# Hybrid decoder layer: the 31-tap depthwise convolution computed by the parity of tokens

## The reference

```
u = conv_val * sigmoid(conv_gate)                      # (B, 2048, 512)
u = causal_depthwise_conv(u, conv_w, conv_b)           # 31 taps, left padded, one filter per channel
uf = u.reshape(B, S, 4, 128)                           # 4 groups of 128 channels
uf = (uf - mean(uf)) * rsqrt(var(uf) + EPS)            # over the 128 channels of a group
y_conv = silu(uf * conv_norm_w + conv_norm_b)
```

## Time and profile before

| | |
|---|---|
| median of 3 runs | 2086.41 us (2086.11 to 2086.6) |
| the profiled execution | 2085.33 us, of which 2083.5 us are the span from the first to the last instruction |
| PE busy | 2067.1 us, 99% |
| DVE busy | 1446.1 us, 69% |
| ACT busy | 912.1 us, 44% |
| POOL busy | 417.2 us, 20% |

### The profile page before, as it was taken

One profiled execution on the slowest core, in us unless ns is written; L12 is line 12 of the kernel. 1 busy time (PEld: TensorE's weight loads), 2 busy tenths in 40 slices (PEclk: granted clock), 3 DMA queues, 4 the chain that ended last, 5 costly groups with the idle time before them and its releaser, 6 DMA issues. The chain is left out here.

```text
span 2083.5 us, 26901 instructions
## 1 busy us (share of the span) xinstructions
PE 2067.1 (99%) x10031; PEld 1734.2 (83%) x10031; DVE 1446.1 (69%) x1993; ACT 912.1 (44%) x1557; POOL 417.2 (20%) x252
## 2 busy tenths in 40 slices
PE   9999999999999999999999999999999999999998
PEld 8897878878788888788888888888788888888887
DVE  6897999989567777886666976666563536624285
ACT  6632434343454445754555654455331313313163
POOL 0000000000002323352332333232353134400012
PEclk9999999999999999999999999999999999999999
DMA  5121212113656875765446755545756455543376
GB/s 204 32 87 47 70 41 81 51 32 105 199 177 195 266 235 171 266 192 167 137 142 191 236 171 156 167 150 189 245 210 259 154 193 202 174 169 126 138 257 218
DMA packets 254144, 338.55 MB, mean 162 GB/s; under 512 B 11584, under 2 KB 195648, under 8 KB 240192
## 3 DMA queue, kind: packets, MB, share of 16 engines
q1 hardware_dynamic: 221376, 315.80, 45.6%
q10 hardware_dynamic: 32384, 20.98, 3.2%
q0 software_dynamic: 256, 0.07, 0.0%
HBM read 225.58 MB, written 111.21 MB: 162 GB/s over the span
## 5 line engine op out<-in xcount | busy, mean ns | idle before, releaser
L1978 PE MATMUL psum<-x_hi,w_hi_P 128*128 128x512 f32 x896 | 349.8, 390 | 3.8 <-DVE x_lo L1922 2.4
L2198 PE MATMUL psum<-w_hi,hid_hi 128*128 128x512 f32 x896 | 348.8, 389 | 1.9 <-DVE hid_lo L2074 1.9
L1978 PE MATMUL psum<-x_lo,w_hi_P 128*128 128x512 f32 x896 | 349.1, 390 | 0.0
L1978 PE MATMUL psum<-x_hi,w_lo_P 128*128 128x512 f32 x896 | 349.1, 390 | 0.0
L2198 PE MATMUL psum<-w_hi,hid_lo 128*128 128x512 f32 x896 | 348.6, 389 | 0.0
L2198 PE MATMUL psum<-w_lo,hid_hi 128*128 128x512 f32 x896 | 348.6, 389 | 0.0
L2074 DVE TENSOR_TENSOR hid_lo<-hid_raw,hid_hi 128x1024 fp32r<-128x1024 f32 x112 | 174.4, 1593 | 211.4 <-ACT hid_hi L2069 211.4
L1891 POOL TENSOR_TENSOR w_raw<-w_raw 128x512 f32<-128x512 f32 x128 | 184.9, 1467 | 395.3 <-DVE w_lo_P L1904 345.8
L2069 ACT ACTIVATE hid_hi<-hid_raw 128x1024 fp32r<-128x1024 f32 x112 | 112.9, 1051 | 343.4 <-DMA hid_raw<-scratch_hid 343.3
L1904 DVE TENSOR_TENSOR w_lo_P<-w_raw,w_hi_P 128x512 fp32r<-128x512 f32 x224 | 184.1, 834 | 98.1 <-ACT w_hi_P L1900 95.5
L1900 ACT ACTIVATE w_hi_P<-w_raw 128x512 fp32r<-128x512 f32 x224 | 136.0, 626 | 236.8 <-PE psum L1978 227.2
(11 more groups left out here) (284 smaller groups left out, 3820.0 us busy)
## 6 DMA issues: line engine op xcount, KB each, us to landing
scratch_hid<-stage SPq DMA_DIRECT2D x224, 256.0 KB, 3.7
hid_raw<-scratch_hid SPq DMA_DIRECT2D x56, 1024.0 KB, 4.9
w_raw<-in_w SPq DMA_DIRECT2D x52, 1024.0 KB, 5.0
w_grain<-in_w SPq DMA_DIRECT2D x48, 512.0 KB, 5.3
x_raw<-scratch_h2s SPq DMA_DIRECT2D x14, 1024.0 KB, 8.4
w_raw<-in_w_in SPq DMA_DIRECT2D x22, 512.0 KB, 3.6
scratch_h2s<-h2s SPq DMA_DIRECT2D x8, 1280.0 KB, 10.1
scratch_qk<-qout ACTq DMA_DIRECT2D x16, 512.0 KB, 3.3
```

The lines of the kernel that those rows point to most:

```text
L1978: mm = nc.tensor.matmul(psum[:, bank_1(op, g), :], l, r, start=kt == 0 and i == 0, stop=kt == 3 and i == 2)
L2198: mm = nc.tensor.matmul(psum[:, bank, :], l, r, start=f == 0 and k == 0, stop=f == NFP - 1 and k == 2)
```

## The change

`u_buf` now holds the even tokens of a unit (with the history of 15 ahead of them) and then the odd ones. Three filters of half length run on 512 outputs each. A: the 16 even-numbered taps on the even stream, 513 outputs, in `a_sum`. B: the 15 odd-numbered taps on the odd stream, in `b_sum`. M: 16 taps, the sums of neighbouring taps, on the sum of the two streams, in the second half of `c_buf`. Even tokens are A + B, odd tokens are M - (A shifted by one + B). For each unit ACT does the first tap of A and of B in `first_taps` and that of M in `pair_tap`; DVE does S (the sum of the streams), 15 taps of A, 14 of B, 15 of M, and E, T, O, the three additions: 48 instructions (`N_STEPS`) of 512 elements (513 for A, 527 for S), each of A, B and M waiting for the one before it in its own chain. `add_weights` sums the taps once. `glu` reads its gate and its PSUM bank with a step of two elements; silu reads halves and writes them interleaved, into `rstd` (unit 7: `c_last`) in place of `c_buf`, so that ACT's square waits for the store of the unit before.

The plan now counts `STEP_COST` = 11.5 for each instruction. The lists that the two versions of it give, worked out from the code:

| unit | 0 | 1 | 2 | 3 | 4 | 5 | 6 | 7 |
|---|---|---|---|---|---|---|---|---|
| last slot of its glu | 7 | 15 | 27 | 31 | 43 | 47 | 67 | 71 |
| CONV_END before | 22 | 29 | 41 | 49 | 60 | 68 | 79 | 87 |
| CONV_END after | 20 | 26 | 37 | 44 | 53 | 61 | 73 | 83 |
| first taps on ACT before | 11 | 21 | 30 | 41 | 49 | 60 | 68 | 78 |
| first taps on ACT after | 11 | 20 | 28 | 37 | 45 | 53 | 67 | 73 |
| pair_tap on ACT after | 12 | 20 | 29 | 37 | 46 | 54 | 67 | 73 |

DVE instructions of the convolution in slots 37 to 44 after the change: 9 (the first of them is O of unit 2, the other eight open unit 3), 2, 8, 3, 7, 9, 4, 7; in slots 50 to 53: 0, 5, 2, 9; in 60 and 61: 7, 6; in 80 to 83: 0, 9, 9, 1. No slot has more than 9; before, none had more than 5.

```diff
-DVE_TAPS = CW - 1
+EVEN, ODD = (CW + 1) // 2, CW // 2
+UH = HALF // 2
+UX = UH + EVEN
...
-TAP_COST = 23
+STEP_COST = 11.5
...
+U_PAIRS_AT, C_LAST_AT = 222848, 99360
...
+def unit_steps():
+
+    out = [("S", 0)]
+    for j in range(1, EVEN):
+        out += [("A", j)] + ([("B", j)] if j < ODD else []) + ([("M", j - 1)] if j > 1 else [])
+    return out + [("E", 0), ("M", EVEN - 1), ("T", 0), ("O", 0)]
+
+
+STEPS = unit_steps()
+N_STEPS = len(STEPS)
+
+
+def step_done(u, kind, j=0):
+
+    return N_STEPS * u + STEPS.index((kind, j)) + 1
...
-                ready = min(ready, DVE_TAPS * u)
-        more = max(0, min(ready - n, room // TAP_COST))
+                ready = min(ready, N_STEPS * u)
+        more = max(0, min(ready - n, int(room // STEP_COST)))
...
-        room = min(room - TAP_COST * more, TAP_COST)
+        room = min(room - STEP_COST * more, STEP_COST)
...
-FIRST_TAP = [max(min(s for s in range(N_SLOTS) if TAPS[s] > DVE_TAPS * u) - 1, glu_end(u)) for u in range(N_UNITS)]
-CONV_END = [min(s for s in range(N_SLOTS) if TAPS[s] >= DVE_TAPS * (u + 1)) for u in range(N_UNITS)]
-
-SECOND_TAP = [max(FIRST_TAP[u], CONV_END[u - 1] if u else 0) for u in range(N_UNITS)]
+CONV_START = [min(s for s in range(N_SLOTS) if TAPS[s] > N_STEPS * u) for u in range(N_UNITS)]
+CONV_END = [min(s for s in range(N_SLOTS) if TAPS[s] >= N_STEPS * (u + 1)) for u in range(N_UNITS)]
+
+FIRST_TAP = [max(CONV_START[u] - 1, glu_end(u), CONV_END[u - 1] if u else 0) for u in range(N_UNITS)]
+
+PAIR_TAP = [max(FIRST_TAP[u], CONV_START[u]) for u in range(N_UNITS)]
...
+        def u_halves(u):
+
+            return u_buf[:, u % U_RING].rearrange("p (a n) -> p a n", a=2)
+
+        def u_pairs(u):
+            return s_late[:] if u else c_buf[:, 1, 0:UX - 1]
+
+        def m_sum(u):
+            return c_buf[:, u % 2, UH:HALF]
+
+        def c_tokens(u):
+
+            return rstd if u < N_UNITS - 1 else c_last
+
+        def pair_weight(g, j):
+            return pairs[:, g * EVEN + j:g * EVEN + j + 1]
...
-            def first_tap(u):
+            def first_taps(u):
                 g = u // 2
                 act.wait_ge(sem["evac"]["dve"], 2 * (u + 1))
                 act.wait_ge(sem["u_head"], u + 1)
-                if u >= 2:
-                    act.wait_ge(sem["c_out"][u % 2], 16 * (u // 2))
-                nc.scalar.activation(c_buf[:, u % 2], u_buf[:, u % U_RING, 0:HALF], ACT.Identity,
+                if u >= 1:
+                    act.wait_ge(sem["tap"], step_done(u - 1, "T"))
+                nc.scalar.activation(a_sum, u_halves(u)[:, 0, 0:UH + 1], ACT.Identity,
                                      scale=par[:, CONV_W + g * CW:CONV_W + g * CW + 1],
                                      bias=par[:, CONV_B + g:CONV_B + g + 1]).then_inc(sem["tap0"], 1)
-
-            def second_tap(u):
+                if u >= 1:
+                    act.wait_ge(sem["tap"], step_done(u - 1, "O"))
+                nc.scalar.activation(b_sum, u_halves(u)[:, 1, 0:UH], ACT.Copy,
+                                     scale=par[:, CONV_W + g * CW + 1:CONV_W + g * CW + 2]).then_inc(sem["tap0"], 1)
+
+            def pair_tap(u):
                 g = u // 2
-                if u >= 1:
-                    act.wait_ge(sem["tap"], DVE_TAPS * u)
-                nc.scalar.activation(c_odd[:], u_buf[:, u % U_RING, 1:1 + HALF], ACT.Copy,
-                                     scale=par[:, CONV_W + g * CW + 1:CONV_W + g * CW + 2]).then_inc(sem["tap0"], 1)
+                act.wait_ge(sem["tap"], step_done(u, "S"))
+                if u >= 2:
+                    act.wait_ge(sem["c_silu"], u - 1)
+                nc.scalar.activation(m_sum(u), u_pairs(u)[:, 0:UH], ACT.Identity, scale=pair_weight(g, 0),
+                                     bias=pairs[:, H * EVEN + g:H * EVEN + g + 1]).then_inc(sem["tap0"], 1)
...
+                        act.wait_ge(sem["c_out"][(u - 1) % 2], 16 * ((u - 1) // 2 + 1))
...
-                    nc.scalar.activation(c_buf[:, u % 2], c_buf[:, u % 2], ACT.Silu, scale=par[:, CN_W + g:CN_W + g + 1],
+                    nc.scalar.activation(c_tokens(u)[:].rearrange("p (n a) -> p a n", a=2),
+                                         c_buf[:, u % 2].rearrange("p (a n) -> p a n", a=2), ACT.Silu,
+                                         scale=par[:, CN_W + g:CN_W + g + 1],
...
-                        first_tap(u)
-                    if SECOND_TAP[u] == s:
-                        second_tap(u)
+                        first_taps(u)
+                    if PAIR_TAP[u] == s:
+                        pair_tap(u)
...
-                nc.vector.scalar_tensor_tensor(out=u_buf[:, u % U_RING, at:at + TB], in0=th[:, (th_uses(s) - 1) % 2, :],
-                                               scalar=1.0, in1=psum[:, banks_of(s)[0], :], op0=ALU.add,
-                                               op1=ALU.mult).then_inc(sem["evac"]["dve"], 1)
...
+                gate, val = (a.rearrange("p (n a) -> p a n", a=2) for a in (th[:, (th_uses(s) - 1) % 2, :], psum[:, banks_of(s)[0], :]))
+                nc.vector.scalar_tensor_tensor(out=u_halves(u)[:, :, at:at + TB // 2], in0=gate, scalar=1.0, in1=val,
+                                               op0=ALU.add, op1=ALU.mult).then_inc(sem["evac"]["dve"], 1)
...
+            def pair_tap(u, j):
+
+                if j == 1:
+                    dve.wait_ge(sem["tap0"], 3 * u + 3)
+                else:
+                    dve.wait_ge(sem["tap"], step_done(u, "M", j - 1))
+                nc.vector.scalar_tensor_tensor(out=m_sum(u), in0=u_pairs(u)[:, j:j + UH], scalar=pair_weight(u // 2, j),
+                                               in1=m_sum(u), op0=ALU.mult, op1=ALU.add).then_inc(sem["tap"], 1)
...
+            def add_pairs(u):
+
+                dve.wait_ge(sem["evac"]["dve"], 2 * (u + 1))
+                if u >= 1:
+                    dve.wait_ge(sem["tap"], step_done(u - 1, "M", EVEN - 1))
+                nc.vector.tensor_tensor(u_pairs(u), u_halves(u)[:, 0, 1:UX], u_halves(u)[:, 1, 0:UX - 1],
+                                        ALU.add).then_inc(sem["tap"], 1)
+
+            def even_tokens(u):
+
+                dve.wait_ge(sem["tap"], step_done(u, "A", EVEN - 1))
+                nc.vector.tensor_tensor(c_buf[:, u % 2, 0:UH], a_sum[:, 0:UH], b_sum, ALU.add).then_inc(sem["tap"], 1)
+
+            def both_sums(u):
+
+                dve.wait_ge(sem["tap"], step_done(u, "E"))
+                nc.vector.tensor_tensor(b_sum, a_sum[:, 1:UH + 1], b_sum, ALU.add).then_inc(sem["tap"], 1)
+
+            def odd_tokens(u):
+
+                dve.wait_ge(sem["tap"], step_done(u, "T"))
+                nc.vector.tensor_tensor(m_sum(u), m_sum(u), b_sum, ALU.subtract).then_inc(sem["tap"], 1)
```

More of the change, by code:

```diff
@@ L185, in tap_plan @@
     for s in range(N_SLOTS):
-        ready = DVE_TAPS * sum(glu_end(u) <= s for u in range(N_UNITS))
+        ready = N_STEPS * sum(glu_end(u) <= s for u in range(N_UNITS))
         if s > FIRST_LOOP:
             room += 100 - 13 * (SLOTS[s][0] == "val") - 76 * len(convs_at(s - 1)) - 22 * len(tiles_split_at(s))
-            room -= 22 * sum(out[s - AT_NORM] >= DVE_TAPS * (u + 1) > out[s - AT_NORM - 1] for u in range(N_UNITS))
-        ends = [min(i for i in range(s) if out[i] >= DVE_TAPS * (u + 1)) for u in range(n // DVE_TAPS)]
+            room -= 22 * sum(out[s - AT_NORM] >= N_STEPS * (u + 1) > out[s - AT_NORM - 1] for u in range(N_UNITS))
+        ends = [min(i for i in range(s) if out[i] >= N_STEPS * (u + 1)) for u in range(n // N_STEPS)]
         for u in range(2, N_UNITS):
             if u - 2 >= len(ends) or s < ends[u - 2] + 9:
-                ready = min(ready, DVE_TAPS * u)
-        more = max(0, min(ready - n, room // TAP_COST))
+                ready = min(ready, N_STEPS * u)
+        more = max(0, min(ready - n, int(room // STEP_COST)))
         for u in range(U_RING, N_UNITS):
             if s + 1 >= glu_slot(u):
-                more = max(more, DVE_TAPS * (u - U_RING + 1) - n)
+                more = max(more, N_STEPS * (u - U_RING + 1) - n)
         n += more
-        room = min(room - TAP_COST * more, TAP_COST)
+        room = min(room - STEP_COST * more, STEP_COST)
         out.append(n)
@@ L514, in tensor @@
                 for u in units_at(s, AT_MEAN):
-                    pe.wait_ge(sem["tap"], DVE_TAPS * (u + 1))
+                    pe.wait_ge(sem["tap"], N_STEPS * (u + 1))
                     if u == 0:
@@ L813, in glu @@
                 u = 2 * g + tb // 2
-                at = CW - 1 + (tb % 2) * TB
+                at = ODD + (tb % 2) * TB // 2
                 if tb % 2 == 0 and u >= U_RING:
-                    dve.wait_ge(sem["tap"], DVE_TAPS * (u - U_RING + 1))
+                    dve.wait_ge(sem["tap"], N_STEPS * (u - U_RING + 1))
                 if tb == 0:
-                    nc.vector.memset(u_buf[:, u % U_RING, 0:CW - 1], 0.0).then_inc(sem["u_head"], 1)
```

(54 more changed lines are left out.)

29 lines of the change are left out of this document (10 added, 19 removed).

## The result

The changed kernel takes 2093.47 us (median of 6 runs, 2091.3 to 2095.18), the one before 2086.4 on the same chips (median of 6, 2084.54 to 2091.52). The ratio is 1.003, 95% interval 1.0017 to 1.0044: slower by 0.3%. It is inside the stated range and on the side to which the larger chance was given; the size was forecast as +4.6 and is +7.1 us.

The account below looks back on a forecast made before the run. PE was taken to bound the kernel, 2067.15 of 2083.5 us busy. Holds of 4.9 us less today's 1.1 of waits, plus 0.8 for hops, gave +4.6: 2089.9 profiled, 2091.0 median, range 2086.0 to 2096.0.

Parts of the forecast that it names:

- DVE's saving: Convolution on DVE: 36.0 us a unit falls to 31.6, saving 4.4 us a unit, 35 us in all.
- A half-length step at 0.66 us: Each 512-element tap on DVE costs 0.66 us start to start, against 1.20 for a 1024-element tap.
- rival (c): Steps of two elements cost: glu and silu double, late glus hold back PSUM banks; 2093.5 us, chance 0.12.
- Rival (a): Hidden, not slower: DVE works ahead enough that chains end before PE's sums; 2086 us, chance 0.28.
- rival (d): DVE's lag accumulates: holds of 1 to 2 us at all eight sums; 2095 us, chance 0.10.
- Unit 3: Opens in slot 37 behind ACT's q/k silu and store; PE held 3.0 us, part maybe at unit 2's second sum.
- Unit 5: Unit 4's root and softplus share slot 58 ahead of ACT's weight split; PE held 0.7 us after slot 62.
- Unit 7: The q/k tap of (7,1) in slot 79 waits behind the store of (7,0); PE held 0.2 us.
- Unit 4: Unit 3's root in slot 49 stands ahead of (4,0)'s ACT tap; PE held 1.0 us after slot 54.
- The sum of holds: PE's holds at the sums of units 3, 4, 5 and 7 total 4.9 us, plus 0.8 for hops.
- The 0.8 added for hops: Allowance of 0.8 us for some 40 waits across engines counted as 0.05 or nothing, and 513-element A steps.
- Slower: Whole kernel slower, bound at 2090.6 us: chance 0.52, from two thirds of the forecast and two rivals.

Follow-up runs that it names:

- the order on ACT alone: Changed kernel with ACT doing a unit's first taps before silu_qk and first_tap_qk in each slot, not behind them: 2089.11 us, ratio to before 1.0013.
- root-last run: Changed kernel with ACT doing each unit's root, except unit 7's, behind the q/k work and first taps of its slot: 2093.66 us, ratio to before 1.0036.
- changed kernel, second execution: The changed kernel run once more with nothing altered: 2093.66 us, ratio to before 1.0039; profiled 2093.26.
- old filters packed: Kernel before, with its 31-tap convolution, and TAP_COST 19 in place of 23: 2110.17 us, ratio to before 1.0114.
- STEP_COST 11: Changed kernel with the plan's price per step 11 in place of 11.5: 2104.65 us, ratio to before 1.009.
- followers later: Changed kernel with all that follows a unit one slot later (distances 2 to 8, not 1 to 7; unit 7's unchanged): 2092.57 us, ratio to before 1.0032.
- STEP_COST 13: Changed kernel with the plan's price per step 13 in place of 11.5: 2093.19 us, ratio to before 1.0034.

## Why the prediction was right, and where it was off

*Right in the mechanism.* PE bounds; DVE's saving (35 us forecast, 32.4 measured) wins only PE's three waits, 1.1 us of gaps: with the old unit ends the matmul behind all the sums starts 1.9 us earlier (558.07 against 559.97), and the whole is 0.8 us faster in the profiled execution and 2 in the medians, and no more. A half-length step at 0.66 us: neighbouring steps start 0.66 apart (the first two of unit 3, 248.41 and 249.08, 0.67). The steps of two elements next to free: `glu` 681 ns, silu 1330 against 1241, 0.1 us more, so rival (c) falls. The Trainium skill (SBUF — State Buffer, note on cachelines) says that a non-contiguous PSUM pattern slows matmuls; for a VectorE read of PSUM at a step of two elements this trace shows nothing of the kind (681 ns against 684). Rival (a), hidden, falls with the holds; rival (d), a small hold at every sum, too: units 0, 1, 2 (first sum) and 6 have none.

*Terms of the sum.* Unit 3, 3.0 us forecast with a part at unit 2's second sum: measured 2.29 + 0.69 = 3.0, and the order on ACT alone removes it. Unit 5, 0.7: measured 1.1; its link, unit 4's root and softplus in one slot ahead of the weight split, is in the trace (DVE waits 4.2 us there), but no run separated it. Unit 7, 0.2: measured 1.17. Unit 4, 1.0: measured 1.70, and its cause was misnamed, as the root-last run shows. The sum of holds was 4.9 + 0.8, measured 7.0. The forecast of each of units 4, 5 and 7 is 0.4 to 1.0 us short. Part of that may be waits across engines in these chains that were put at 0.05 or nothing (0.3 to 0.5 us before a q/k tap, three times) and first taps on ACT of 0.8 us (L672, L685) for 0.7; this was not separated. The 0.8 added for hops was too small.

*The terms that were missing.* Each hold was priced at its gap. It costs some 0.25 us more, and in some executions the matmuls behind it run at half the clock, 1.5 us more. The forecast of the profiled execution, 2089.9, came within 1.4 us of 2091.31, with 0.9 us that phase C gave back. From there to the median 2093.47 are 2.2 us, and the forecast added only the 1.1 by which the median of before lay above its profile.

*Chances.* Slower had 0.52 and same 0.45; the forecast of +4.6 us lay just over the 4.2 us that make the difference. That it came out as slower owes something to the terms left out. The measured interval, 0.17% to 0.44%, shows a slowdown, but it does not quite exclude one under the 0.2% that was the bound.

## What to carry to other kernels

Where one engine is busy 99%, time saved on another is worth only the waits that it ends; before spending it, ask what starts earlier because of it and whose queue that lands in. A hand-written schedule has to be priced and placed again after a change, and the cheap check is to add up the in-order queues from one fixed event (the end of a slot on the bound engine) to the next wait of that engine. The half-length filters with the old unit ends (STEP_COST 14) are the version to keep: 2084.25 us, 0.12% under the kernel before and 0.4% under the changed one.

## What the runs showed of the hardware that was not expected

A gap of TensorE costs more than its length: with gaps of 0.69, 1.70 and 2.29 us ahead of the sums, the stretch from the matmul before them to the one behind them grew from 1.55 us to 2.49, 3.51 and 4.10, some 0.26 us more than the gap each time.

TensorE's granted clock fell to 1.2 GHz behind some holds and not behind others. The mean granted clock over the 3.9 us from the start of the sums:

| hold, us | run | clock |
|---|---|---|
| 2.15 | root last, unit 4 | 1.00 |
| 2.27 | changed kernel, second execution | 0.59 |
| 2.27 | root last, unit 3 | 0.69 |
| 2.29 | changed kernel, first execution | 1.00 |
| 2.88 | old filters packed | 1.00 |
| 3.42 | STEP_COST 11 | 1.00 |
| 3.93 | old filters packed | 0.59 |
| 4.03 | old filters packed | 0.66 |
| 4.24 | old filters packed | 0.50 |
| 5.18 | followers later | 0.50 |
| 5.38 | STEP_COST 13 | 0.58 |
| 10.93 | STEP_COST 11 | 0.52 |

From 2.15 to 3.42 us it went either way, not in order of length, and even both ways at the same place of the same kernel; the six holds from 3.93 us on all had it. The same shows early in phase C: every execution has one wait of 2.2 us for `x_lo` (near 855 us), and behind it the clock is 0.60 in the kernel before and 1.00 in the run with the first taps ahead. A fall costs these four matmuls at most 1.8 us (3.78 - 1.98), no more behind 10.93 us than behind 5.18; part of it can fall on the matmuls behind them, as in the root-last run, where the four last 2.44 us and the next six run at 0.50 too (293.20 to 296.50). Two executions of one program can so differ by 1.5 us with equal waits.
